# Held weight buffers in a mixture of experts: where the split work stands in each engine's order

## The reference

```python
def swiglu(h, wg, wu, wd):
    return (jax.nn.silu(h @ wg) * (h @ wu)) @ wd

def moe_swiglu(h, w_router, wg, wu, wd):
    logits = (h @ w_router).astype(jnp.float32)
    top_v, top_i = lax.top_k(logits, TOP_K)
    top_w = jax.nn.softmax(top_v, axis=-1)
    gates = ...                                # (tokens, 8), two non-zeros a row
    y = jnp.zeros_like(h)
    for e in range(N_EXPERTS):
        y = y + gates[..., e:e + 1] * swiglu(h, wg[e], wu[e], wd[e])
    return y
```

## Time and profile before

| | |
|---|---|
| median of 3 runs | 1383.79 us (1382.92 to 1390.79) |
| the profiled execution | 1383.09 us, span 1381.2 us, mean granted clock 0.965 |
| share of the chain that ended last | PE 82%, DMA 7%, DVE 6% |
| busy | PE 1300.3, DVE 718.9, ACT 525.1, POOL 120.5 us |
| mixture of experts | from about 745 us to 1360 us of the span |

### The profile page before, as it was taken

One profiled execution on the slowest core, in us unless ns is written; L12 is line 12 of the kernel. 1 busy time (PEld: TensorE's weight loads), 2 busy tenths in 40 slices (PEclk: granted clock), 3 DMA queues, 4 the chain that ended last, 5 costly groups with the idle time before them and its releaser, 6 DMA issues.

```text
span 1381.2 us, 17263 instructions
## 1 busy us (share of the span) xinstructions
PE 1300.3 (94%) x6503; PEld 959.1 (69%) x6504; DVE 718.9 (52%) x1021; ACT 525.1 (38%) x632; POOL 120.5 (9%) x119
## 2 busy tenths in 40 slices
PE   5999999999999999999999799999789999999994
PEld 2555459999999854776558686654356778888882
DVE  1101565342432426554246874623335668898888
ACT  0101043332422232332125463522324557777772
POOL 0510005000000051000000000101002010202020
PEclk8999999999999999999996899999998999999997
DMA  9985474443342375511216774768966879999993
GB/s 366 359 323 214 174 283 138 153 164 109 108 165 91 117 277 179 211 33 70 98 67 232 242 247 162 255 244 317 367 233 213 310 281 378 368 371 392 372 352 150
DMA packets 125355, 317.09 MB, mean 230 GB/s; under 512 B 12931, under 2 KB 47078, under 8 KB 124774
## 3 DMA queue, kind: packets, MB, share of 16 engines
q1 hardware_dynamic: 119264, 295.00, 58.3%
q0 software_dynamic: 5744, 21.07, 5.0%
q10 hardware_dynamic: 278, 0.10, 0.0%
HBM read 306.37 MB, written 9.76 MB: 229 GB/s over the span
## 4 chain that ended last, share of the span: by engine, by line
PE 82%; DMA 7%; DVE 6%; SPq 2%; ACT 2%; issue 1%; DVEq 0%; ACTq 0%
PE ps L2526 9%; PE ps L2528 8%; PE ps L2527 8%; PE ps L2224 8%; PE ps L2226 8%; PE ps L2225 8%; PE ps L2189 7%; PE ps L2126 6%; PE ps L2532 5%; DMA sb_expert_raw<-in_moe_w_up 4%; PE ps L2316 3%; DVE sb_expert_w L1755 2%; DMA sb_ring<-in_ev_w_in 2%; PE ps L2086 2%; PE ps L2418 1%
## 5 line engine op out<-in xcount | busy, mean ns | idle before, releaser
L1755 DVE TENSOR_TENSOR sb_expert_w<-sb_expert_raw,sb_expert_w 128x1792 fp32r<-128x1792 f32 (+1 forms) x210 | 339.0, 1648 | 130.4 <-ACT sb_expert_w L1204 129.6
L1204 ACT CAST sb_expert_w<-sb_expert_raw 128x1792 fp32r<-128x1792 f32 (+1 forms) x210 | 287.1, 1392 | 178.9 <-DMA sb_expert_raw<-in_moe_w_down 88.4
L2526 PE MATMUL ps<-sb_expert_w,sb_expert_x 128*128 128x448 f32 x448 | 171.9, 384 | 27.5 <-DVE sb_expert_w L1755 16.7
L2527 PE MATMUL ps<-sb_expert_w,sb_expert_x 128*128 128x448 f32 x448 | 166.9, 373 | 0.0
L2528 PE MATMUL ps<-sb_expert_w,sb_expert_x 128*128 128x448 f32 x448 | 166.8, 372 | 0.0
L2526 PEld LDWEIGHTS ps<-sb_expert_w,sb_expert_x 128*128 128x128 f32 x448 | 86.5, 193 | 57.6 <-issue 34.2
L2224 PE MATMUL ps<-sb_split_acts,sb_split_weights 128*128 128x384 f32 x352 | 118.7, 337 | 0.4 <-issue 0.4
L2226 PE MATMUL ps<-sb_split_acts,sb_split_weights 128*128 128x384 f32 x352 | 118.4, 336 | 0.0
L2225 PE MATMUL ps<-sb_split_acts,sb_split_weights 128*128 128x384 f32 x352 | 118.4, 336 | 0.0
L2528 PEld LDWEIGHTS ps<-sb_expert_w,sb_expert_x 128*128 128x128 f32 x448 | 86.3, 193 | 7.7
L2527 PEld LDWEIGHTS ps<-sb_expert_w,sb_expert_x 128*128 128x128 f32 x448 | 86.6, 193 | 7.1
(11 more groups left out here) (334 smaller groups left out, 1830.5 us busy)
## 6 DMA issues: line engine op xcount, KB each, us to landing
sb_expert_raw<-in_moe_w_gate SPq DMA_DIRECT2D x128, 448.0 KB, 6.4
sb_expert_raw<-in_moe_w_up SPq DMA_DIRECT2D x128, 448.0 KB, 7.7
sb_expert_raw<-in_moe_w_down SPq DMA_DIRECT2D x112, 512.0 KB, 5.1
sb_ring<-in_ada_w SPq DMA_DIRECT2D x14, 3072.0 KB, 17.0
sb_ring<-in_ffn_w_gate SPq DMA_DIRECT2D x44, 256.0 KB, 3.7
sb_ring<-in_ffn_w_up SPq DMA_DIRECT2D x44, 256.0 KB, 4.7
sb_ring<-in_ffn_w_down SPq DMA_DIRECT2D x22, 512.0 KB, 6.2
sb_ring<-in_ev_w_in SPq DMA_DIRECT2D x4, 2048.0 KB, 14.9
```

Source lines behind the costliest of these rows:

```text
L1204: nc.scalar.copy(EWS[r][:, 0, 0:w], ERAW[:, r, 0:w]).then_inc(e_hi, 1)
L1755: V.tensor_tensor(EWS[r][:, 1, 0:w], ERAW[:, r, 0:w], EWS[r][:, 0, 0:w].bitcast(F32), ALU.subtract)\
L2526: first = mm(out, lh, rh, start=start, stop=False)
L2527: mm(out, lh, rl, start=False, stop=False)
```

## The change

Four edits. (1) The table in two parts: DVE first writes only the experts of the eight passes (`by_pass`) and raises `tab_ready` to 1, which the engines now wait for (`order_ready`); the arithmetic of the left-over blocks and `more` moves behind `x_low(1)`, ahead of the split of pass 0's last down piece, and `more` is read just before the loop. (2) `ahead`: next to held buffers (p or the pass before in KEPT) ACT and DVE split one piece of the next stretch before the SiLU, not four. (3) In a pass with two blocks the PE does two pieces for the primary block, then the same two for the secondary one. (4) Pass 2 is a full split block of 128 rows, so that KEPT becomes passes 1 and 3, and its `spread` goes from 5 to 3.

```diff
@@ PASSES
-    (7, half(), None),
+    (7, full(), None),
@@ lookahead
+        def ahead(p, before):
+            return 1 if p in KEPT or before in KEPT else 4
@@ more_items
+        def order_ready(eng):
+            eng.wait_ge(tab_ready, 1)
         def more_items(eng):
-            eng.wait_ge(tab_ready, 1)
+            eng.wait_ge(tab_ready, 2)
@@ pass_highs (ACT)
-                turn = KD + spread(before) + 4
-                expert_highs(p, 0, KD + 4)
+                more = ahead(p, before)
+                turn = KD + spread(before) + more
+                expert_highs(p, 0, KD + more)
                 gate_silu(p, 0)
-                expert_highs(p, KD + 4, turn)
+                expert_highs(p, KD + more, turn)
                 h_high(p, 0)
-                expert_highs(p, turn, KD + EB + 4)
+                expert_highs(p, turn, KD + EB + more)
                 y_out(before)
-                expert_highs(p, KD + EB + 4, 2 * KD + EB + 4)
+                expert_highs(p, KD + EB + more, 2 * KD + EB + more)
                 gate_silu(p, 1)
...
@@ pass_lows (DVE): the same bounds
...
@@ table (DVE)
+            def by_pass():
+                ch(V.tensor_tensor(above, across(IX[:, 0:NE]), down_(cst("iota", 1)[:, 0:NE]), ALU.is_equal))
+                ch(V.tensor_tensor(above, above, across(cst("iota", 1)[:, 0:NE]), ALU.mult))
+                ch(V.tensor_reduce(FIRST, above, AX.X, ALU.add))
+                V.tensor_copy(TAB[:, 1:1 + NE], FIRST).then_inc(tab_ready, 1)
...
             by_rank(IX[:, 0:NE], "pass_of")
-            by_rank(CAP, "rows_of")
-            expert_lows(0, 4, 5)
-            left_over()
-            expert_lows(0, 5, 6)
+            by_pass()
+            order_ready(dve)
+            expert_lows(0, 4, 6)
             dve.wait_ge(h_stored, 16 * NG)
-            passes_of(0, cand("cand_expert"))
             expert_lows(0, 6, 7)
-            passes_of(1, FROM)
-            V.tensor_copy(TAB[:, :], TF).then_inc(tab_ready, 1)
-            more = more_items(dve)
             picked(0)
             select(1)
...
             x_low(1)
-            expert_lows(0, 2 * KD + 6, FIRST_N)
+            by_rank(CAP, "rows_of")
+            expert_lows(0, 2 * KD + 6, FIRST_N - 1)
+            left_over()
+            passes_of(0, cand("cand_expert"))
+            passes_of(1, FROM)
+            V.tensor_copy(TAB[:, 0:1], TF[:, 0:1])
+            V.tensor_copy(TAB[:, 1 + NE:], TF[:, 1 + NE:]).then_inc(tab_ready, 1)
+            expert_lows(0, FIRST_N - 1, FIRST_N)
@@ gate_up (PE)
+                for k in range(0, KD, 2):
+                    primary(k)
+                    primary(k + 1)
                     if more_rows:
+                        secondary(k)
+                        secondary(k + 1)
@@ down (PE)
-                for j in range(spread(p), EB):
-                    primary(j)
+                for j in range(spread(p), EB, 2):
+                    pair = range(j, min(j + 2, EB))
+                    for i in pair:
+                        primary(i)
                     if more_rows:
-                        secondary(j)
+                        for i in pair:
+                            secondary(i)
```

More of the change, by code:

```diff
@@ L786, in _ @@
                 expert_down(e_piece(0, 2 * KD + b), 0, b)
-            more = more_items(sp)
+            order_ready(sp)
             def pass_loads(p, e_before, e):
@@ L803, in _ @@
                 e_before = e
+            more = more_items(sp)
             with sp.Fori(0, more) as j:
@@ L961, in _ @@
             pool.wait_ge(h_stored, 16 * NG)
-            more = more_items(pool)
             n = 0
@@ L969, in _ @@
                     n += 1 + (p - 1 in SECOND)
+            more = more_items(pool)
             with pool.Fori(0, more) as j:
@@ L1807, in _ @@
             row = lambda a, n: MS[0:1, a:a + n]
+            FIRST = row(800, 8)
             KEY, RANK, IX, CAP, STARTS, FROM = row(300, 8), row(308, 8), row(316, CANDS), row(340, 8), row(348, 16), row(364, CANDS)
@@ L1923, in pass_lows @@
                 after = p + 1 if isinstance(p, int) else (p[0], p[1] + 1)
-                turn = KD + spread(before) + 4
+                more = ahead(p, before)
+                turn = KD + spread(before) + more
                 expert_lows(p, 0, 4)
                 select(after)
-                expert_lows(p, 4, KD + 4)
+                expert_lows(p, 4, KD + more)
                 hidden(p, 0)
-                expert_lows(p, KD + 4, turn)
+                expert_lows(p, KD + more, turn)
                 h_low(p, 0)
                 picked(after)
-                expert_lows(p, turn, 2 * KD + EB + 4)
+                expert_lows(p, turn, 2 * KD + EB + more)
                 hidden(p, 1)
-                turn = min(ITEM_N, 2 * KD + EB + spread(p) + 4)
-                expert_lows(p, 2 * KD + EB + 4, turn)
+                turn = min(ITEM_N, 2 * KD + EB + spread(p) + more)
+                expert_lows(p, 2 * KD + EB + more, turn)
                 h_low(p, 1)
@@ L2575, in gate_up, with primary @@
                 x = XEW if p in WHOLE else XES
-                for k in range(KD):
+                def primary(k):
                     piece = e_piece(p, c0 + k)
@@ L2583, in gate_up, with secondary @@
                         last.then_inc(gu_ps, 1)
-                    if more_rows:
[L2585 to L2593, removed]
+                    elif not more_rows:
+                        last.then_inc(e_used, 1)
+                def secondary(k):
+                    if k == 0 and u == 0:
+                        tokens_split(pe, p, 1)
+                    elif k == 0:
+                        hidden_split(pe, p, 0, 1)
+                    _, last = gate_up_block(more_rows, XES2, e_piece(p, c0 + k).r, k)
+                    last.then_inc(gu_ps if k == KD - 1 else e_used, 1)
+                for k in range(0, KD, 2):
+                    primary(k)
+                    primary(k + 1)
+                    if more_rows:
+                        secondary(k)
+                        secondary(k + 1)
             def down_block(b, h, col, r, start, stop):
@@ L2691, in _ @@
             gate_up(0, 0, 0, False)
-            more = more_items(pe)
+            order_ready(pe)
             pick(1)
@@ L2704, in _ @@
                 pass_products(p, p - 1)
+            more = more_items(pe)
             with pe.Fori(0, more) as j:
```

5 lines of the change are left out of this document (3 added, 2 removed).

## The result

The changed kernel takes 1411.43 us (median of 4 runs, 1402.55 to 1416.04) beside 1385.13 of the kernel before on the same chip: ratio 1.0207, interval 1.0164 to 1.025. The profiled execution took 1409.58 with a span of 1407.7, 26.5 more than the one before. Forecast 1398, range 1376 to 1410: the direction was right, and the time lies just above the range. That it is slower is clear of the scatter; whether by more than 2% is not, since the interval reaches down to 1.0164.

What follows compares the result with a forecast made beforehand. The PE was taken as the bound, its chain 82% of the span. Table +0.9, pairs -8, full block -4, lookahead +24 gave +13, stretch by stretch +13.4; with clock +1.4, 1383.1 becomes 1398, range 1376 to 1410.

Steps and rivals of the forecast that it cites:

- The table, +0.9: Pass 0: piece 7's wait and low clock go (-6.9), a wait ahead of the last down piece comes (+6.4, clock +1.4).
- hidden table: Rival, 1390 us: DVE finishes the moved table arithmetic before the PE needs piece 22, so 6.4 + 1.4 come back; chance 0.10.
- The pairs, -8: Two pieces at a time halve the block changes, 0.3 us each: gate pairs 4.8, down pairs about 3.
- The full block, -4 by itself: Pass 2 split: gate stretches +6.2, first down stretch -3.7, second -6.9; together -4.4, kept at -4.
- The lookahead, +24: One piece of lookahead, passes 1 to 4: new split waits 33, less 5.7 replaced load waits, less 3 not paid twice.
- (a): PE waits for the second down piece, whose split stands behind the SiLU: 8 in passes 2 and 4, 5.6 in 1 and 3.
- (b): PE waits behind the transposes, the next splits standing behind `h_high`, `x_high`, `h_low`, `picked` or `x_low`: 11.3 us in all.
- (c): Second gate stretches: `y_out(before)` now stands behind piece 15's high, not 18's; waits 2.2, 2.0, 2.3, 1.4 in passes 1 to 4: 8.
- I take one, since most lie near the harmless end: +1.4: Clock after waits of 2.0 to 2.5 us: seven such waits at 1.4 each give 0 to 10; one counted.
- low clock, 1408: Rival: four or more new waits are followed by 1.2 GHz, or two neighbouring ones count as one long one; chance 0.15.
- (d): New waits replace present transfer waits as loads catch up: 1.24 in pass 1, 3.7 in pass 4, 0.8 at its start: -5.7.
- faster, 1373: the splits are late anyway: Rival: the lookahead costs nothing, since ACT mostly waits for landed weights; -10, range 1366 to 1379, chance 0.20.

Runs made afterwards that it cites:

- filled form: Changed kernel plus eight and nine dummy matmuls ahead of the second and fifth down pieces in passes 2 and 4: 1412.72 us, again 1409.9.
- the version with three pieces: All four edits but three pieces of lookahead and the left-over arithmetic in pass 1, against the kernel before: 1370.69 us, ratio 0.9905; again 1371.7, 0.992.

## Why the forecast was right in its direction and too low by 13 us

**The table, +0.9.** The mechanism was right: the wait of 5.44 went, one of 5.96 came (6.4 forecast), low clock behind it, and pass 1 starts at 820.55 for 820.35. The size is +0.2 in the profile and +3.0 by the medians of the table alone (its interval is +1.5 to +7.5, just above the forecast). The rival "hidden table" fell with the row at 817.83.

**The pairs, -8.** Too large. The first gate stretch of pass 1 lost 1.3 (35.99 to 34.68), close to four changes of block at 0.3. Alone the whole is -4.8, with -8.2 to -1.9 as its interval, so 8 is at its edge. Beside one piece of lookahead no gain is left to see; the pairs take away the secondary piece that covered part of a scaling wait.

**The full block, -4 by itself.** In sign right, -2.4, within the scatter. What I added up pass by pass beside the lookahead, +9.5 for pass 2, measured +15.1.

**The lookahead, +24.** Its waits came where and as long as worked out:

| waits | forecast | measured in passes 1 to 4 |
|---|---|---|
| (a) second down piece | 13.6 | 1.29, 1.30; 1.86, 1.88; 1.09, 1.11; 1.86, 1.87: 12.3 |
| (b) behind transposes | 11.3 | 1.89; 1.37; 2.11, 0.48; 0.79, 2.12: 8.8 |
| (c) behind `y_out` | 8 | 2.29, 1.79, 2.33, 0.69: 7.1 |
| sum | 33 less 3 | 28.2 |

The rest of the 33.2 in the chain are 1.65, 2.18, 0.42 and 0.81, all ahead of gate pieces of pass 4 and all behind a high that itself waited for its transfer (the first 1.65 at 1106.12; the 2.18 at 1146.43 is the low of the high at 1142.54 above, which idled 3.44 for its load). The experiment that takes the lookahead out shows that this part carries the loss.

**The step that failed: "I take one, since most lie near the harmless end: +1.4".** The prediction said that a wait of 2.0 to 2.5 is followed by 1.2 GHz either never or at 1.4 each, and took one of seven. Six in passes 1 to 4 were. At 1.5 each that is 9.2 instead of 1.4, 7.8 of the 13 that separate 1398 from 1411. I had leaned on four waits that had left the clock at 1.00, but those were 1.05, 0.23, 0.52 and 1.88 long, three of them much shorter than the ones I was adding. The rows of the right length were divided: 2.27 in pass 2 had gone low, 1.88 in pass 4 and 2.10 ahead of its first piece, just before the second window of the earlier trace rows, had not. In the two profiles of the changed kernel 11 of the 20 waits of 1.8 to 2.3 in passes 1 to 4 went low. So nothing in the rows supported one in seven, and how many would go low in one execution is in part chance. The rival "low clock, 1408" named this mechanism at four or more waits and came closest.

**The second step: (d), the waits that the new ones replace, -5.7.** I had the waits for loads in the long stretch of pass 4, 3.7, vanish, since the loads would catch up meanwhile. Pass 1's 1.24 did vanish. Pass 4's did not: 2.18, 0.42 and 0.81 are 3.4, and the stretch is 42.92 for 39.3 at a clock of 1.00. What the loads waited for is in the rows of the load queue. In the last down stretch of pass 3, which begins at 1125.94, its waits that end on the PE are (three views, of 1134 to 1137, 1137 to 1141 and 1141 to 1145)

```profile
SPq L702 <- PE ps L2554: 11.7, 1, 11.7
SPq L693 <- PE ps L2554: 2.6, 1, 2.6
SPq L693 <- PE ps L2554: 1.9, 1, 1.9
```

and the load behind the first, and the PE's row that runs when its slot comes free, are

```profile
1134.54 0.33 SPq L702 DMA_DIRECT2D sb_expert_raw<-in_moe_w_down  x1
...
1133.71 1.50 PE L2554 MATMUL ps<-sb_expert_raw,sb_second_h 128*32 128x256 f32 x24
```

(L702 issues a down piece, L693 a gate piece.) The DMA engines moved nothing from 1125.94 to 1133.94. These are held buffers, freed only when the PE has done the short block's matmuls, behind the transposes. Before, the same load went out 6.5 behind the start of the stretch (1115.16 for 1108.69), now 8.6, and 1.86 of the 2.1 is the PE's own new wait ahead of the second down piece. So the loads could not catch up during that wait: it held them back too. That this accounts for the whole of the waits further on is not shown; no kernel tested it alone.

Passes 1 to 4 took 27.7 more where their forecast sums to 12.5; of the 15.2 beyond it the clock has 9.2 and pass 4's loads 3.6. The other 2.4 lie mostly in pass 2, and I have not traced them to one piece.

Two slips of the working changed little. The terms of pass 2 sum to 9.7, not 9.5. And of the shares 1.03 and 1.04 only the first belongs to a stretch named there: the one with 8.08 of 16.90 has 0.87, and its wait of 8.82 ended on DVE's L1778, the row numbers of the next pass (`picked`), which stood behind a split that was late by its load.

The rival "faster, 1373: the splits are late anyway" fell with ACT's row at 1126.96: three landed pieces, rounded in a row behind the SiLU.

That the edits add up would have been wrong. Alone they give +12.2, -4.8, -2.4 and +3.0, in sum +8; together +26.3. The passes of the prediction had part of this in (pass 2 at +9.5), and the four round terms could not.

The Trainium skill's "DMA: Bandwidth & Descriptors" (Where 436 GB/s comes from) would hold the core to about 358 GB/s, which it works out as a stack's 716 GB/s over two cores; this kernel runs on one alone. The changed kernel's row at 929.94 has 385 over 19.7 us with the PE never waiting: the trace does not agree, and the page's +1.6 did not come.

## What to carry to other kernels

Where in-order engines run a written-out list, price each bound by what stands between two steps of the engine that waits. Here two pieces of lookahead instead of one, at the activation, the turned rows and the output scaling together, were worth 27 us, and three with the side work moved gave the fastest kernel. A new wait of about 2 us on the PE is to be priced at its length plus the stretch at 1.2 GHz that may follow (here 1.5 more, behind 11 of 20). Its length does not decide whether one follows, so it is a range and not a number. Where a buffer is freed by the engine that waits, its wait holds the next loads back as well. Edits that take the same slack (fuller blocks, fewer changes, less lookahead) are to be priced together, and side work on an engine put where the PE has the longest piece ahead of it.

## What the runs showed of the hardware

Waits of one length had different clocks behind them from one execution to the next: 1.87 at the same matmul was followed by 0.57 and by 1.00 (the windows at 1172 and 1173 above). Those of 2.28 to 2.37 ahead of the second piece of the second gate stretches of passes 1 and 3 were followed by 1.2 GHz in every profile of the changed kernel and of its filled form. Yet two longer ones, 2.44 at 1078.14 and 2.68 at 1115.67 in the second profile of the version with three pieces, were not, so the length of the wait alone does not tell:

```profile
1078.14:1082.14 4.00, 4.00 (x20) 3.69 (x21) 3.69 (x2) 2.84 (x3) 0.00 (x0) 1.00 1.03 413
1115.67:1119.67 4.00, 3.69 (x17) 3.07 (x18) 2.25 (x2) 2.85 (x3) 0.00 (x0) 1.00 1.03 418
```

One program's times scatter over 12 us (the kernel before: 1377.06 to 1388.67 in 27 runs), and they follow the mean granted clock of the run: 0.93 us less for each 0.001 more, correlation -0.84; 1.11 and -0.88 in the next 29, 2.05 and -0.94 in the next 7, 0.77 and -0.68 in the last 17. The difference of 3.0 of the table alone showed with 11 runs beside 29, and one of 2.4 (the full block alone) did not with 10 beside 27.

The DMA engines moved 385 GB/s over 19.7 us on this one core while the PE did not wait.
